# Copying and adding the finished attention output at the start of an item, and square and root ahead of the gate copy

## What is computed

```python
def _diff_attend(q1, q2, k1, k2, v, q_pos, k_pos, lam):
    scale = ATT_HD ** -0.5
    mask = k_pos[None, :] <= q_pos[:, None]
    def probs(q, k):
        s = jnp.einsum('bqhd,bkhd->bhqk', q.astype(jnp.float32), k.astype(jnp.float32)) * scale
        return jax.nn.softmax(jnp.where(mask, s, NEG_INF), axis=-1)
    w = probs(q1, k1) - lam * probs(q2, k2)
    return jnp.einsum('bhqk,bkhe->bqhe', w, v.astype(jnp.float32))
...
    o = _attend(q1, q2, k_all[..., :ATT_HD], k_all[..., ATT_HD:], v_all, q_pos, k_pos, lam)
    o = _rmsnorm(o, lw['subln_g'], eps=1e-5) * (1.0 - lam_init)
...
    f = (jax.nn.silu(h @ lw['ffn_w_gate']) * (h @ lw['ffn_w_up'])) @ lw['ffn_w_down']
```

## Time and profile before

| | |
|---|---|
| median of 3 runs | 3150.6 us (3144.96 to 3151.73) |
| the profiled execution | 3149.44 us |
| its span | 3147.7 us |
| granted TensorE clock, mean over the span | 0.973 of full speed |
| busy PE / DVE / ACT / POOL | 94% / 57% / 44% / 7% |

### The profile page before, as it was taken

The page is one execution under the profiler, slowest core; times in us unless marked ns, Lnnn a source line. Parts: engine busy times, 40 slices in busy tenths (PEclk is TensorE's granted clock), DMA queues, the critical chain, the costliest instruction groups (busy, mean ns, idle before and its releaser), DMA issues.

```text
span 3147.7 us, 38465 instructions
## 1 busy us (share of the span) xinstructions
PE 2961.2 (94%) x14384; PEld 2408.5 (77%) x14384; DVE 1779.7 (57%) x2858; ACT 1377.4 (44%) x2501; POOL 220.6 (7%) x314
## 2 busy tenths in 40 slices
PE   6999999768999999999999999999999999999997
PEld 5788787657667877877787778777888877787875
DVE  5767745467436666565565565655666555334454
ACT  4655635354234455454444444544444444222233
POOL 0101110100000100001111000001010000000000
PEclk9999989879999999999999999999999999999998
DMA  5546342837654443553443335434432344232221
GB/s 163 176 140 233 131 139 68 239 135 223 194 141 113 112 123 106 168 148 107 131 118 97 101 103 175 147 98 125 112 106 77 104 155 134 85 99 81 84 75 54
DMA packets 377577, 402.59 MB, mean 128 GB/s; under 512 B 25642, under 2 KB 277846, under 8 KB 377393
## 3 DMA queue, kind: packets, MB, share of 16 engines
q1 hardware_dynamic: 360624, 341.32, 36.6%
q0 software_dynamic: 16768, 58.81, 5.2%
HBM read 341.19 MB, written 58.91 MB: 127 GB/s over the span
## 4 chain that ended last, share of the span: by engine, by line
PE 61%; DVE 11%; ACT 3%; issue 2%; DMA 0%; SPq 0%; DVEq 0%; ACTq 0%; POOL 0%; POOLq 0%
PE c_bank L2600 49%; PE b_S L2892 3%; PE b_WT L2904 2%; DVE c_w L2280 2%; PE b_O L2918 2%; DVE b_m L2480 1%; PE b_S L2609 1%; PE b_O L2609 1%; ACT c_junk L2052 1%; DVE c_rows L2291 1%; DVE c_rows L2298 1%; PE b_S L2872 1%; PE b_O L2920 1%; DVE c_act L2392 1%; DVE b_p L2487 1%
## 5 line engine op out<-in xcount | busy, mean ns | idle before, releaser
L2600 PE MATMUL c_bank<-c_hT,c_w 128*128 128x512 f32 (+1 forms) x4416 | 1041.0, 390 | 15.3 <-DVE c_hT L2318 15.3
L2600 PEld LDWEIGHTS c_bank<-c_hT,c_w 128*128 128x128 f32 x4416 | 804.7, 192 | 173.4 <-issue 18.2
L2280 DVE TENSOR_TENSOR c_w<-c_raw,c_w 128x1024 fp32r<-128x1024 f32 x334 | 405.3, 1220 | 196.1 <-ACT c_w L2031 194.8
L2600 PE MATMUL c_bank<-c_w,c_fT 128*128 128x512 f32 x2112 | 506.5, 393 | 0.0
L2031 ACT ACTIVATE c_w<-c_raw 128x1024 fp32r<-128x1024 f32 x334 | 351.1, 1054 | 286.4 <-PE c_bank L2600 246.4
L2600 PEld LDWEIGHTS c_bank<-c_w,c_fT 128*128 128x128 f32 x2112 | 391.7, 188 | 87.0 <-issue 3.4
L2209 ACT ACTIVATE b_p<-b_S,b_nm 128x512 f32<-128x512 f32 (+3 forms) x288 | 180.2, 631 | 522.6 <-DVE b_nm L2481 522.6
L891 PE MATMUL a_bank<-a_w,a_hT 128*128 128x512 f32 (+1 forms) x1224 | 300.4, 401 | 0.0
L2600 PE MATMUL c_bank<-c_w,c_hT 128*128 128x512 f32 x1152 | 271.7, 394 | 7.7 <-DVE c_w L2280 4.0
L891 PEld LDWEIGHTS a_bank<-a_w,a_hT 128*128 128x128 f32 (+1 forms) x1224 | 220.8, 183 | 61.3 <-issue 3.8
L2600 PEld LDWEIGHTS c_bank<-c_w,c_hT 128*128 128x128 f32 x1152 | 219.0, 191 | 55.1 <-DVE c_w L2280 4.4
(11 more groups left out here) (363 smaller groups left out, 3375.4 us busy)
## 6 DMA issues: line engine op xcount, KB each, us to landing
c_raw<-in_ffn_w_gate SPq DMA_DIRECT2D x88, 512.0 KB, 4.8
c_raw<-in_ffn_w_up SPq DMA_DIRECT2D x88, 512.0 KB, 4.2
c_raw<-in_ffn_w_down SPq DMA_DIRECT2D x88, 512.0 KB, 4.0
a_raw<-in_w_in SPq DMA_DIRECT2D x40, 1024.0 KB, 5.2
b_k<-split_kT SPq DMA_DIRECT2D x72, 256.0 KB, 4.9
b_v<-split_v SPq DMA_DIRECT2D x36, 512.0 KB, 3.6
c_raw<-in_w_out SPq DMA_DIRECT2D x32, 512.0 KB, 5.0
c_raw<-in_ple_w_gate SPq DMA_DIRECT2D x32, 512.0 KB, 4.4
```

What stands on the lines that cost most here:

```text
L2280: V.tensor_tensor(w[:, e[1] % SLOTS, 1], raw[:, n % RAW], w[:, e[1] % SLOTS, 0].bitcast(F32), ALU.subtract).then_inc(split_ready, 1)
L2600: ins = T.matmul(out, lhs(k, a), rhs(k, b), start=first and k == 0 and n == 0, stop=end and k == blocks - 1 and n == 2)
```

## The change

In an item with a finished tile the copy `ob` of ScalarE and the sum `o` of VectorE move from the end of the item to its start: on ScalarE right behind the copy-out of a head and ahead of the tanh, on VectorE ahead of everything. The square and the root stay late in ScalarE's item but now stand ahead of the gate copy. The order of VectorE's other operations (weighted sum, maximum of a tile) stays. No wait is dropped: each moved instruction takes its waits with it.

```diff
@@ ScalarE, start of the item
+                x = finished(n, 1)
+                if x is not None:
+                    act.wait_ge(pv_done, last_step[x] + 1)
+                    wait_if_any(act, o_ready, x)
+                    A.activation(ob[:], O[:, 0, 1], ACT.Copy).then_inc(ob_ready, 1)
                 if was == ("mix0", 3):
@@ ScalarE, end of the item
-                if was[0] in ("up", "far"):
-                    b = was[1]
-                    bank, count = job[j, "up", b]
-                    act.wait_ge(acc_free[bank], count)
-                    A.activation(fT[:, b % 8, 0], act1[:, b % 2], ACT.Copy).then_inc(f_hi, 1)
                 x = finished(n, 1)
                 if x is not None:
-                    act.wait_ge(pv_done, last_step[x] + 1)
-                    wait_if_any(act, o_ready, x)
-                    A.activation(ob[:], O[:, 0, 1], ACT.Copy).then_inc(ob_ready, 1)
                     act.wait_ge(o_ready, x + 1)
                     wait_if_any(act, osq_ready, x)
                     A.activation(ojunk[:], o[:, x % 4], ACT.Square, accum_out=oss[:, x % 4:x % 4 + 1]).then_inc(osq_ready, 1)
                     if x % 4 == 3:
                         act.wait_ge(osq_ready, x + 1)
                         A.activation(oss[:], oss[:], ACT.Sqrt, bias=eps[:, 2:3], scale=1.0 / P).then_inc(ostd_ready, 1)
+                if was[0] in ("up", "far"):
+                    b = was[1]
+                    bank, count = job[j, "up", b]
+                    act.wait_ge(acc_free[bank], count)
+                    A.activation(fT[:, b % 8, 0], act1[:, b % 2], ACT.Copy).then_inc(f_hi, 1)
@@ VectorE, start of the item
+                x = finished(n, 1)
+                if x is not None:
+                    dve.wait_ge(ob_ready, x + 1)
+                    if x >= 4:
+                        dve.wait_ge(o_turned, x // 4)
+                    V.tensor_tensor(o[:, x % 4], O[:, 0, 0], ob[:], ALU.add).then_inc(o_ready, 1)
@@ VectorE, end of the item
                 x = finished(n, 1)
-                if x is not None:
-                    dve.wait_ge(ob_ready, x + 1)
-                    if x >= 4:
-                        dve.wait_ge(o_turned, x // 4)
-                    V.tensor_tensor(o[:, x % 4], O[:, 0, 0], ob[:], ALU.add).then_inc(o_ready, 1)
```

## The result

The changed kernel takes 3202.87 us (median of 5, 3199.19 to 3206.44), the kernel before, run beside it, 3148.98 us (median of 5, 3144.96 to 3151.73). The ratio is 1.017, with a 95% interval of 1.0157 to 1.0183: slower by 54 us. The profiled execution of after took 3199.19 us, its span is 3197.4 us, 49.8 more than before.

What follows compares the result with a forecast made beforehand. TensorE, 94% busy, was taken as the bound, so only its waits count. Order terms summing to +45.2 us plus +11.8 for the clock raised the profiled 3149.4 to 3206.4, median 3208 us, range 3178 to 3236.

Steps and rivals of the forecast that it cites:

- Gate places: 19 items with a finished tile where VectorE owes gate products: transposes 0.97 to 1.66 us later each, 24.0 us in sum.
- Places without gate products: 21 items with a finished tile but no gate products owed: transposes about 1.00 us later each, 20.6 us in sum.
- tiles 7 and 9: Items following the end of a down block: VectorE's four row additions start 2.1 us later, 4.2 us for both.
- The heads' ends: Chains to finished heads' transposes: six without gate products gain 6.2 us; with gate-place gains and two losses, net gain 4.6.
- Tile 15: Head's end with five small coefficient operations behind VectorE's gate remainder: its head's transposes estimated 2.2 us later.
- tile 31: Head's end with no value step in its item: its chain starts later, an estimated loss of 0.9 us.
- tiles 3, 11 and 19: Heads ending in gate places: the head's transposes come 0.5 us sooner each, -1.5 us in sum.
- The clock: Longer TensorE pauses at 21 places: four in ten followed by a clock fall costing 1.60 us, +11.8 us net.
- A: Rival: early copy and addition find ScalarE and VectorE idle, so waiting order costs nothing: 3138 us, chance 0.04.
- B: Rival: only gate places pay, VectorE's slack absorbing the late weight copy elsewhere: +34 us, 3185 us, chance 0.12.
- C: Rival: the clock falls nearly each time, with further idling behind: 3230 us or above, chance 0.09.
- D: Rival: losses and gains cancel, needing a delay of about 0.2 us per tile: 3150 us, chance 0.03.

Runs made afterwards that it cites:

- late_both: Changed kernel with ScalarE's copy moved to just ahead of the exponentials and VectorE's sum behind the weighted sum: 3144.47 us, 0.9990 of the kernel before.
- act_early: Changed kernel with only VectorE's sum moved, to behind the weighted sum, ScalarE's copy staying at the item's start: 3199.48 us.
- front_only: Changed kernel with the gate copy put back ahead of square and root, copy and sum staying at the item's start: 3203.74 us.
- tail: Kernel before with only square and root moved ahead of the gate copy, and VectorE's sum ahead of its gate remainder: 3153.52 us.
- late_gate: As late_both, but with the gate copy also put back ahead of the square: 3138.92 us, 0.9968 of the kernel before.
- after_again: The changed kernel unaltered, profiled a second time: 3198.95 us.
- dve_early: Changed kernel with only ScalarE's copy moved, to just ahead of the exponentials, VectorE's sum staying first in the item: 3191.25 us.
- double: Changed kernel with ScalarE's waiting copy made twice in a row, the first into a scratch tile: 3220.61 us.

## Why the prediction was right, and where it was off

**Bound and direction: right.** TensorE's idle time is the time of this kernel, and the stretch in question grew by 48.2 us from its first scores to its last value products; the other 1.6 of the spans' difference lie before and behind it (+4.0 and -2.4), where nothing was changed.

**Gate places: right, 24.0 predicted, 25.6 measured.** The four kinds are late by 1.05, 1.29, 1.52 and 1.74 us where 0.97, 1.20, 1.43 and 1.66 were worked out. The gate products start at S+1.08 and not S+0.99: tanh's start at S+0.37 and its 0.59 were right, but 0.12 lie between its end and theirs; the sum had put 0.02 there. late_both and act_early show the mechanism: with the tanh ahead of the copy nothing is lost, with the copy ahead and no sum on VectorE all of it.

**Places without gate products: right, 20.6 predicted, 22.2 measured.** Most are late by the 1.0 us of the forecast (the remainder starts at S+1.46 against S+1.45); six (tiles 18, 37, 38, 40 to 42) by 0.2 to 0.35 more, since their remainder takes 1.40 to 1.56 us, as in the rows of tile 41, where GpSimd is already at work when it starts. Tile 46 cost about 1.4 (1.0 predicted), tiles 7 and 9 together 4.0 (4.2), tiles 20 and 35 nothing, as said.

**The heads' ends: right, a net 4.6 predicted, 5.7 measured.** The waits are 6.8 in place of 12.5 us. The six heads in plain items lost their 1.0 each. Tile 15 waits 2.1 longer (2.2 predicted; 1.3 of it by the moved gate copy, since front_only has 2.34 us there against 3.62) and tile 31 0.7 (0.9). Of tiles 3, 11 and 19 the forecast took 0.5 off each; tiles 3 and 19 gave 0.3 and 0.5, and tile 11 all of its 1.6, because the fall behind its pause made the products ahead of its head's transposes 1.6 us longer (the 4.58 us above), time in which the normalisation was finished. In act_early, where the clock did not fall there, the waits for b_o are 8.3 us, 6 times. The forecast left unasked whether the order with the gate copy first would be better still; front_only, tail and late_gate show that it is, by some 3 us.

**The clock: the term that was mis-sized.** "So 21 x 0.4 x 1.6", less one, made +11.8 us. The price per fall was right (1.58 us in the rows of tile 11, 1.60 forecast), its frequency was not. In the trace of after only two of the 21 pauses were followed by a fall. A third new fall stands behind tile 15's wait of 3.62 us, and three falls that the trace of before had at other places (1010, 2007 and 2075 us) are gone, so in the two profiled executions the term is about zero: the waits above sum to 25.6 + 22.2 + 1.4 + 4.0 - 5.7 = 47.5, and one down item that was late in before got 0.6 back, which leaves 1.3 of the 48.2 us for the clock and all scatter. Over all profiles with the full delay (after, after_again, front_only, act_early) it was 10 of 82 (in act_early tiles 7 and 9 have no such pause). The error is in the sample: the ten pauses of before that gave "four of ten" were 1.6 to 2.5 us long and stood in different surroundings, while 58 of the 82 new ones are of 1.76 to 1.85 us and one of them was followed by a fall. A smaller miss: for tiles 7 and 9 the prediction had pauses of 2.5 us, and they are 1.83 and 1.84, since a part of the delay falls earlier in the item, where the block products wait for the row additions (0.40 us at 1078.82).

**The median.** The forecast of the median came within 5 us, and part of that is luck. Between the profiled executions the time grew by 49.8 us where 57.0 were forecast; the medians beside each other differ by 53.9. The profiled execution of after was the shortest of its five. The 36 executions of before beside the experiments have a mean span of 3147.4 us and a granted clock of 0.9736 over the span; the 13 of after, front_only and act_early have 3200.1 and 0.9716. Among those of before a granted clock lower by 0.001 goes with a span longer by 1.9 us. By that 0.002 of clock are some 4 us, an estimate; it leaves 49 of the 52.7 us between the two means, close to the 47 us of waits. That would be about a third of the term, but it is not shown that the lengthened pauses cost it. The twelve executions of late_both, which has no such pauses, have 0.9715 too. By the traces TensorE stood at the lower clock for 41 us in the attention stretch of before, 44 in after and 51 in each of after_again, front_only and act_early, but also 48 in tail and late_both; and outside the stretch the same time goes from 125 to 142 us among these seven. What the pauses cost by the clock, over many executions, stays open.

**The rivals.** A (the order of waiting costs nothing) fell: the lead of VectorE is nil in gate places, as the 35 waits had said. B (only gate places pay) fell with the 22.2 us of the plain ones. C (falls nearly each time) fell with two of 21; the five pauses of 3.0 us in dve_early, each with a fall, show where it would have held. D (losses and gains cancel) fell with the 54 us.

## What to carry to other kernels

On an engine that works through its list in order, an instruction that waits is worth its wait to everything queued behind it; the engine's low busy share says nothing of that. Put it behind all that doesn't need what it waits for, on its own engine and on each engine that waits for it in turn: here the copy at the same moment but behind tanh and weight copy, and the sum behind the weighted sum, turned +54 us into -11. When following a move, list every instruction between the old and the new place in each kind of item, the rare ones too (against its expectation the c_pT copy cost dve_early some 6 us, 1.3 in each of five items, and more by the clock).

## What the runs showed of the hardware that was not expected

- How often a pause of TensorE is followed by a fall of the clock from 2.4 to 1.2 GHz went with its length and its place: 1 of 62 pauses of 1.76 to 1.85 us, 9 of 20 of 1.85 to 1.90 us, 6 of 23 of 1.93 to 2.10 us, 5 of 5 of about 3.0 us (after, after_again, front_only, act_early, double and dve_early); while in before one of 1.64 us was followed by a fall and one of 1.61 us not. The 20 pauses with nine falls are all at the five places with c_pT transposes, so the place may matter as much as the length; this wasn't taken apart. A fall cost 1.57 to 1.60 us, except the long one of tile 32 in dve_early.
- Where the weight remainder of VectorE (128x1024 elements, two inputs) met the weighting of b_p on GpSimd (128x512), the one that started later paid. In before the GpSimd operation started 0.28 to 0.30 us behind the remainder in 23 places: the remainder took its 1.22 us and GpSimd's operation 1.5 us in place of 0.7. In after it had started 0.20 to 0.38 us ahead in eight places: it took at most its 0.7 us, and the remainder 1.28 to 1.56 us. So the change, by moving the remainder, also moved who pays; six of the 21 plain places were later by it.
- Of two ScalarE copies of 0.28 us back to back, the second cost only 0.16 to 0.18 us (double: it starts 0.18 us after the first, and the tanh 0.16 after it).
